# Queries' and keys' weights ahead of the second modulation piece, and their first products moved with them, in a two-layer hybrid backbone step

## What is computed

```python
mod = (jax.nn.silu(cond) @ lw['w_ada'] + lw['b_ada'])[:, None, :]
shift1, scale1, gate1, shift2, scale2, gate2 = jnp.split(mod, 6, axis=-1)
h = rmsnorm(x, lw['norm_mix']) * (1 + scale1) + shift1
rq, rk, rv, rg, dq, dk, dv, cq, ckv, kpe = jnp.split(h @ lw['w_in'], offsets, axis=-1)
```

## Time and profile before

| | |
|---|---|
| median of three runs | 1336.48 us |
| the profiled execution, its own time | 1338.24 us |
| its span in the profile | 1336.3 us |
| TensorE matmuls busy | 1225.3 us, 92% |
| VectorE, ScalarE busy | 280.3 us (21%), 239.4 us (18%) |
| loaded from memory | 493.60 MB, 371 GB/s over the span |
| chain that ended last | TensorE 68%, DMA 24%, VectorE 4% |

### The profile page before, as it was taken

How to read it: one execution, slowest core, us unless ns; L and a number is a source line. 1 busy time by engine, 2 the same in 40 slices (tenths; PEclk the granted TensorE clock), 3 DMA queues, 4 the chain that set the end, 5 groups by cost and what they waited for, 6 DMA issues and landing times.

```text
span 1336.3 us, 22734 instructions
## 1 busy us (share of the span) xinstructions
PE 1225.3 (92%) x9596; PEld 835.2 (62%) x9596; DVE 280.3 (21%) x720; ACT 239.4 (18%) x533; POOL 2.8 (0%) x13
## 2 busy tenths in 40 slices
PE   7999999999998889888999999999999889888986
PEld 4566686667765565556565668766767466556554
DVE  1252362111111010101034425401101010101012
ACT  2363131110010001010134521311010001010102
POOL 0000000000000000000000000000000000000000
PEclk9999999999999999889999999999999899889989
DMA  9888849999999999999956663999999999999992
GB/s 385 335 318 339 352 188 422 399 422 421 421 421 422 422 422 422 420 421 422 395 218 247 251 233 149 418 420 421 421 420 421 421 422 422 422 422 421 423 420 105
DMA packets 80657, 496.58 MB, mean 372 GB/s; under 512 B 10576, under 2 KB 12880, under 8 KB 24784
## 3 DMA queue, kind: packets, MB, share of 16 engines
q1 hardware_dynamic: 76528, 493.63, 90.1%
q10 hardware_dynamic: 4064, 2.00, 0.5%
HBM read 493.60 MB, written 2.00 MB: 371 GB/s over the span
## 4 chain that ended last, share of the span: by engine, by line
PE 68%; DMA 24%; DVE 4%; SPq 2%; issue 1%; ACT 1%; DVEq 0%; ACTq 0%
DMA dn<-in_exp_w_down 18%; PE PS L2205 15%; PE PS L2241 13%; PE PS L2135 8%; PE PS L2142 7%; PE PS L1709 7%; PE PS L2041 4%; DMA gu<-in_exp_w_gate 4%; PE PS L1651 2%; PE PS L1619 2%; DMA gu<-in_w_in 1%; PE PS L2090 1%; PE PS L1832 1%; PE PS L1843 1%; PE PS L2181 1%
## 5 line engine op out<-in xcount | busy, mean ns | idle before, releaser
L2205 PE MATMUL PS<-gu,arena 128*32 128x256 f32 (+1 forms) x3072 | 313.4, 380 | 0.0
L2241 PE MATMUL PS<-arena 128*64 128x512 f32 (+1 forms) x336 | 180.0, 686 | 63.7 <-DMA dn<-in_exp_w_down 62.1
L2205 PEld LDWEIGHTS PS<-gu,arena 128*32 128x32 f32 (+1 forms) x3072 | 182.6, 117 | 79.0 <-issue 18.0
L2241 PE MATMUL PS<-dn,arena 128*32 128x512 f32 (+1 forms) x688 | 187.7, 640 | 0.0
L2135 PE MATMUL PS<-arena 128*128 128x128 f32 x1408 | 176.3, 278 | 0.5 <-ACT arena L1042 0.5
L2135 PEld LDWEIGHTS PS<-arena 128*128 128x128 f32 x1408 | 164.1, 192 | 17.9 <-issue 16.7
L2142 PE MATMUL PS<-arena 128*128 128x256 f32 x704 | 160.2, 380 | 1.4 <-ACT arena L1025 1.4
L2205 PE MATMUL PS<-arena 128*64 128x256 f32 (+1 forms) x672 | 152.0, 379 | 0.0
L2142 PEld LDWEIGHTS PS<-arena 128*128 128x128 f32 x704 | 130.2, 190 | 20.5 <-ACT arena L1025 3.2
L1530 DVE TENSOR_TENSOR arena<-arena,PS 128x256 f32<-128x256 f32 x44 | 18.5, 421 | 563.1 <-ACT arena L1038 563.1
L1025 ACT ACTIVATE arena<-PS 128x512 f32<-128x512 f32 x88 | 52.6, 597 | 462.6 <-PE PS L2241 462.6
(11 more groups left out here) (264 smaller groups left out, 1023.9 us busy)
## 6 DMA issues: line engine op xcount, KB each, us to landing
gu<-in_exp_w_gate SPq DMA_DIRECT2D x106, 1024.0 KB, 15.7
gu<-in_exp_w_up SPq DMA_DIRECT2D x86, 1024.0 KB, 17.6
dn<-in_exp_w_down SPq DMA_DIRECT2D x86, 1024.0 KB, 18.6
arena<-in_exp_w_up SPq DMA_DIRECT2D x42, 1024.0 KB, 14.6
arena<-in_exp_w_down SPq DMA_DIRECT2D x42, 1024.0 KB, 16.2
gu<-in_w_ada SPq DMA_DIRECT2D x20, 2048.0 KB, 8.9
xh<-in_exp_w_gate SPq DMA_DIRECT2D x22, 1024.0 KB, 11.4
gu<-in_w_in SPq DMA_DIRECT2D x8, 2048.0 KB, 13.1
```

Of the source, the lines that this page charges most:

```text
L2205: ins = mmul(PS[w * h:w * h + w, 5, FF * half:FF * half + FF], xg[:, k, w * h:w * h + w], weights[half][:, k], start=(k == 0), stop=(k == ...
L2241: ins = mmul(PS[w * h:w * h + w, 7 - n, :], hidT[:, j * P + w * h:j * P + w * h + w], weights[:, j, 512 * n:512 * n + 512], start=(j == 0) ...
```

## The change

In the load order `w_in` 2 moves one place ahead, to stand before modulation piece 1. In TensorE's order the call for the queries and keys of chunks 0 to 3 is split. Chunks 0 and 1 are taken right behind `chunks_select(0)`, ahead of `chunks(1)`, and chunks 2 and 3 right behind the values of chunks 0 and 1. No instruction is added or removed.

```diff
-LOADED_EARLY = [(("w_in", 0, 2), ("chunks", 0, 2)), (("w_in", 0, 3), ("chunks", 0, 2)), (("mla", 0, 0), ("ada", 0, 6)),
+LOADED_EARLY = [(("w_in", 0, 2), ("chunks", 0, 1)), (("w_in", 0, 3), ("chunks", 0, 2)), (("mla", 0, 0), ("ada", 0, 6)),
                 (("w_in", 0, 0), ("ada", 0, 10)), (("w_in", 0, 1), ("ada", 1, 0))]
...
                     chunks(0)
                     chunks_select(0)
+                    queries_and_keys((0, 1))
                     chunks(1)
                     chunks_select(1)
-                    queries_and_keys((0, 1, 2, 3))
                     values_and_latent((0, 1))
+                    queries_and_keys((2, 3))
                     chunks(2)
                     values_and_latent((2,))
                     chunks_select(2)
```

## The result

The changed kernel is slower by a little. Over 20 runs of each, the median is 1340.03 us against 1337.24 us before. The ratio is 1.0022 with a 95% interval of 1.0014 to 1.0030, that is +2.9 us (1.9 to 4.0). A second comparison of the same two kernels, on another chip, gave 1.0026 (1.0017 to 1.0036), that is +3.5 us (2.3 to 4.8), with a median of 1341.06 us over 12 runs. Forecast were +1.2 us, "within 0.3%" and 1335.4 to 1340.6 us. The first time lies in the range, at its upper end; that of the second comparison lies 0.5 us past it.

What follows compares the result with a forecast made beforehand. Bound taken: TensorE's unbroken work at the beginning. Idle and half-clock time ahead of `chunks(2)` goes from 4.1 us to 5.4 (0.72 + 2.4 + 0.72 + 1.55); `chunks(2)` 1.2 us later, so 1336.48 + 1.2 = 1337.7 us, range 1335.4 to 1340.6.

Steps and rivals of the forecast that it cites:

- The load that seemed to bound the beginning: Ahead of the first queries and keys: TensorE had idled only 0.24 us for the load of `w_in` 2.
- The landings: Weight loads: `w_in` 2 at 16.7 us, modulation piece 1 at 21.6, `w_in` 3 at 27.0, piece 2 at 33.4.
- The new wait: Behind `chunks_select(0)`: TensorE stands still 2.4 us for `hT`, until 19.5 us.
- The wait ahead of the second select: TensorE's wait for `rada` there becomes 0.72 us instead of 1.45.
- The clock: At the first queries and keys: 3.4 us at half clock, costing 1.55 us against 1.7 before.
- it moves, it doesn't vanish: The clock's fall comes earlier, at the first products, costing 1.55 us against 1.7 before.
- The sum: `chunks(2)` starts at about 35.2 us instead of 33.97, 1.2 us later.
- Carried to the end: From `chunks(2)` to the kernel's end: the 1.2 us passes one to one, bounds 0 and 1.2.
- its slowest case: The two-fall case, 1339.4 us; the range's upper end was this plus 1.2 us, 1340.6.
- No fall: Beginning: no half clock after the change, `chunks(2)` at 34.15, +0.2 us, 1336.7; chance 0.22 together with no effect.
- Two falls in the beginning: Half clock behind 19.5 us and again behind 26.6 to 28.2: +2.9 us, 1339.4; chance 0.17.
- Modulation piece 3 late: At `chunks(3)`: piece lands at 45.8, TensorE stands still 4.3 us; +5.5 us in all, 1342.0; chance 0.07.

Runs made afterwards that it cites:

- e5: Kernel before, with VectorE norming only chunks 0 and 1 ahead of the first bias and gain; measured 1.0000 (0.9990 to 1.0010) of the kernel before.
- e4: Changed kernel, with VectorE norming only chunks 0 and 1 ahead of the first bias and gain; measured 1.0002 (0.9992 to 1.0012) of the kernel before.
- e8: The changed kernel as it is, run and profiled again on another chip; measured 1.0026 (1.0017 to 1.0036) of the kernel before.
- e11: Changed kernel plus two unused wide matmuls (0.86 us) in TensorE's wait for the ranking of experts, both layers; 1.0017 (1.0006 to 1.0028) of the kernel before.
- e7: Kernel before plus two unused wide matmuls (0.86 us) behind `chunks(1)`, in the 1.45 us wait for `rada`; 0.9995 (0.9986 to 1.0004) of the kernel before.
- e3: Changed kernel plus four unused wide matmuls (1.7 us) in its new wait behind the first select; 1.0024 (1.0012 to 1.0036) of the kernel before.
- e6: Kernel before plus ten unused wide matmuls (4.3 us) just ahead of `chunks(2)`; 1.0052 (1.0038 to 1.0067) of the kernel before, +7.0 us.
- e9: Kernel before plus four unused wide matmuls (1.7 us) just ahead of `chunks(2)`; 1.0018 (1.0008 to 1.0028) of the kernel before, +2.4 us.
- e10: Kernel before plus twenty unused wide matmuls (8.5 us) just ahead of `chunks(2)`; 1.0102 (1.0089 to 1.0115) of the kernel before, +13.6 us.
- e1: Kernel before with only the new load order, TensorE's order kept; 1.0035 (1.0022 to 1.0047) of the kernel before, +4.7 us.
- e2: Kernel before with only TensorE's new order, load order kept; 1.0044 (1.0029 to 1.0060) of the kernel before, +5.9 us.
- e12: Kernel before plus unused matmuls both behind `chunks(1)` and in the wait for the ranking, both layers; 1.0011 (0.9999 to 1.0024) of the kernel before.

## Why the prediction was right, and where it was off

**The load that seemed to bound the beginning.** Right: 0.24 us was all that it gave. `e5` shows how waits stand behind each other there: shortening one fed another.

**The landings.** Right to 0.3 us for `w_in` 2 (16.6 against 16.7), piece 1 (21.6) and `w_in` 3 (26.9 against 27.0). Piece 2 came at 31.9 instead of 33.4 us, probably since piece 3 was no longer issued into the queue beside it; nobody waited for either.

**The new wait.** Right in size (2.48 against 2.4 us), in where it stands and in what releases it, and `e4` shows its cause: without 1.45 us of it the changed kernel can't be told from the kernel before. It ended at 19.87 us and not at 19.5, since that whole execution began 0.3 us later (`chunks(0)` at 13.70 against 13.39). The wait ahead of the second select was 0.72 us, as forecast.

**The clock.** The fall moved to the first products, as forecast, and cost 1.65 us (5.27 less 3.62) against 1.55. In `e8` it was 1.5, and in `e11`, which begins like the changed kernel, 2.9 us (6.47 less 3.62):

```profile
19.07 6.47 PE L1832 MATMUL PS<-xh,gu 128*128 128x256 f32 x16 [2.48 <-ACT xh L857]
```

What was wrong is the other side of the sum: I credited the kernel before with a loss of 1.7 us to its own fall. `e7` shows that all but 0.4 us of it lay in the shadow of the load of piece 2. The sum itself went by the times of both and doesn't suffer from that, but "it moves, it doesn't vanish" hid what mattered: the fall moved from where a load covered it to where only TensorE's own work follows. In the profiles that is 0.4 us before (`e7`) against 1.5 us after (35.69 less the 34.15 of `e3`); the median of `e3` doesn't bear it out.

**The sum.** +1.2 us at `chunks(2)` was too small. Three profiles with the changed beginning have their place at 35.69, 35.18 and 36.09 us (mean 35.65), four with the old one at 33.90, 34.03, 33.97 and 33.56 (the last three are `e6`, `e9` and `e10`, up to where the delay is put in; mean 33.87). The difference is 1.8 us, or 1.6 us if each place is counted from the same execution's `chunks(0)`. The term that was too small is the half clock, taken from one execution: it cost 1.65, 1.5 and 2.9 us, on average 2.0 against 1.55. It lasted 3.4 us in the first two and 6.8 us in `e11`.

**Carried to the end.** Right up to 169 us. Behind it the measured 2.9 us (1.9 to 4.0) leaves about 1 us more than 1.8. That the median lies in the range in spite of it is in part luck: without the 1.2 us by which the range was stretched past its slowest case it would lie outside, as the median of the second comparison does even so. I had bounded the pass-through by 0 and 1, and left out that it could exceed 1. The second fall at the routing, 1.7 us in both profiles of the changed kernel, is of a size to make it, if it comes in a good part of its executions; that share isn't known. The 4.5 us more at 1.2 GHz, over all runs, point the same way without saying where. The prediction also took it that nothing further on would change the 1.2 us; in the profiles the distance to the kernel before goes from 3.5 to 4.6 us (changed kernel) and from 2.7 to 1.0 us (`e8`) between the first expert and layer 1.

**The rivals.** No fall: not seen in any profile of the changed kernel, but made by `e3`, with the place at 34.15 us, just what that rival had worked out. Two falls in the beginning: not seen with this beginning, only in `e4`; `e11` shows one of double length instead. Modulation piece 3 late: wrong; its 19.2 us belonged to the queue, and it landed 4.0 us ahead of its use. The range held the time by what it had been stretched to on the slow side; the case that the time came nearest to, 1339.4, was forecast by another mechanism.

## What to carry to other kernels

Ahead of taking work forward, ask what its other operand waits for: the weights were moved to be there at 16.6 us, but the activations came at 19.8, and what had covered the gap was the work moved behind. In such an order a load and the use of it have to move together; either alone cost 4.7 to 5.9 us here. And a slow stretch seen in the profile counts only for the part that no load behind it would have claimed anyway: 1.7 us of half clock were worth 0.4 at the next landing. Last, one profile is one execution: those of `e4`, `e8` and `e3` were the slowest, the fastest and one of the fast of their twelve runs, and small differences have to be taken from the medians.

## What the runs showed of the hardware

The granted clock fell to 0.50 (1.2 GHz) in or behind waits of TensorE and stayed there for 3.4 us in the profile before and for 6.8 us in `e11`, but for about 10 us in those of `e1` and `e2`, whose waits for a load were 3.8 and 5.8 us. It didn't fall where 1.7 us (`e3`) or 0.9 us (`e7`) of wide matmuls stood in the wait. This agrees with the section "HAM oscillation — how this bites in real kernels" of the Trainium skill's page "TensorE: Matmul & The Clock Gate", that the burst behind a wait pays for it.

TensorE stood still for 0.5 to 2.1 us with no releaser in the trace, at places far behind the edit, in seven kernels to which something had been added or in which an order had been changed (`e1`, `e5`, `e6`, `e7`, `e9`, `e10`, `e12`). Four of these stalls stand where the kernel before idles for 0.26 us. An experiment that adds instructions may not be neutral, whatever it fills.
